# Rounding nine weight chunks by a casting DMA of GpSimd, and starting four tiles of a down projection before a wait

## The reference, cut to what matters

```python
u = rmsnorm(h, mix_norm)
(aq, ak, av, gq, gk, gv, gr, g_low, gate_a, gate_b) = split(u @ w_in)
ya = window_sink_attention(aq, ak, av, sinks)           # softmax over blocks of 64 tokens
yb = gated_linear_attention(gq, gk, gv, log_a)          # a recurrence in chunks of 64
...
h = h + 0.5 * (silu(x @ w_gate) * (x @ w_up)) @ w_down  # 1024 -> 2816 -> 1024
```

## Time and profile before

| what | value |
|---|---|
| median of 3 runs | 1890.07 us |
| the profiled execution | 1890.56 us, span 1888.4 us |
| TensorE matmul busy | 98% of the span |
| VectorE, ScalarE, GpSimd busy | 65%, 43%, 5% |
| granted TensorE clock | 0.999 of full speed |
| DMA | 110 GB/s on average |

### The profile page before, as it was taken

How to read it: one execution, slowest core, us unless ns; L and a number is a source line. 1 busy time by engine, 2 the same in 40 slices (tenths; PEclk the granted TensorE clock), 3 DMA queues, 4 the chain that set the end, 5 groups by cost and what they waited for, 6 DMA issues and landing times.

```text
span 1888.4 us, 27498 instructions
## 1 busy us (share of the span) xinstructions
PE 1858.1 (98%) x11675; PEld 1606.4 (85%) x11675; DVE 1225.5 (65%) x1498; ACT 820.8 (43%) x1154; POOL 99.5 (5%) x105
## 2 busy tenths in 40 slices
PE   8999999999999999999999999999999999999998
PEld 3788878877888888799999999888778878998998
DVE  8667743458657567587694785764554567695784
ACT  4544543336435345264452454554333354352442
POOL 0021000002000000000100100000000000110100
PEclk9999999999999999999999999999999999999999
DMA  8454423222244333222543443211122233544441
GB/s 337 154 187 157 156 80 123 89 89 68 73 123 123 98 120 95 90 74 72 139 123 107 115 121 101 90 59 46 68 83 95 90 95 95 134 112 123 116 121 66
DMA packets 66344, 208.12 MB, mean 110 GB/s; under 512 B 4512, under 2 KB 32704, under 8 KB 51376
## 3 DMA queue, kind: packets, MB, share of 16 engines
q1 hardware_dynamic: 36656, 173.55, 26.9%
q0 software_dynamic: 29568, 32.84, 8.5%
HBM read 204.27 MB, written 2.10 MB: 109 GB/s over the span
## 4 chain that ended last, share of the span: by engine, by line
PE 92%; DVE 5%; ACT 2%; issue 1%; DMA 0%; POOL 0%; DVEq 0%; ACTq 0%; POOLq 0%
PE PS L833 90%; PE PS L1000 1%; DVE W_lo L2305 1%; ACT W_hi L1675 0%; DVE N L2959 0%; ACT N L1675 0%; DVE N L2954 0%; DVE T L3037 0%; DVE N L2918 0%; DVE N L2949 0%; ACT H_hi L1675 0%; ACT X L1675 0%; DMA X<-in_xT 0%; DVE N L2333 0%; PE PS L1292 0%
## 5 line engine op out<-in xcount | busy, mean ns | idle before, releaser
L1675 ACT ACTIVATE W_hi<-W_raw 128x2048 fp32r<-128x2048 f32 (+3 forms) x158 | 289.9, 1836 | 351.4 <-PE PS L833 328.2
L833 PE MATMUL PS<-H_hi,W_hi 128*128 128x512 f32 (+2 forms) x1296 | 428.0, 345 | 5.4 <-POOL H_lo L801 2.4
L833 PE MATMUL PS<-H_lo,W_hi 128*128 128x512 f32 (+2 forms) x1296 | 425.8, 344 | 0.0
L833 PE MATMUL PS<-H_hi,W_lo 128*128 128x512 f32 (+2 forms) x1272 | 422.9, 347 | 0.0
L2305 DVE TENSOR_TENSOR W_lo<-W_raw,W_hi 128x2048 fp32r<-128x2048 f32 (+2 forms) x107 | 236.9, 2214 | 102.6 <-ACT W_hi L1675 102.4
L833 PEld LDWEIGHTS PS<-H_hi,W_hi 128*128 128x128 f32 x1296 | 236.1, 188 | 40.8 <-issue 4.4
L833 PEld LDWEIGHTS PS<-H_lo,W_hi 128*128 128x128 f32 x1296 | 235.6, 188 | 30.3 <-issue 0.7
L833 PEld LDWEIGHTS PS<-H_hi,W_lo 128*128 128x128 f32 x1272 | 232.0, 188 | 28.9 <-issue 0.7
L833 PE MATMUL PS<-G_hi,W_hi 128*128 128x264 f32 (+2 forms) x736 | 215.7, 332 | 2.1 <-DVE G_lo L3024 1.6
L833 PE MATMUL PS<-G_lo,W_hi 128*128 128x264 f32 (+2 forms) x736 | 216.2, 333 | 0.0
L833 PE MATMUL PS<-G_hi,W_lo 128*128 128x264 f32 (+2 forms) x736 | 215.6, 332 | 0.0
(11 more groups left out here) (362 smaller groups left out, 3456.7 us busy)
## 6 DMA issues: line engine op xcount, KB each, us to landing
W_raw<-in_wts SPq DMA_DIRECT2D x116, 1024.0 KB, 4.9
ring<-in_wada POOLq DMA_DIRECT2D x32, 512.0 KB, 3.9
W_raw<-in_wdown SPq DMA_DIRECT2D x12, 1024.0 KB, 5.0
W_raw<-in_wts POOLq DMA_DIRECT2D x45, 256.0 KB, 4.4
W_raw<-in_wdown SPq DMA_DIRECT2D x12, 768.0 KB, 4.4
W_raw<-in_wdown SPq DMA_DIRECT2D x12, 640.0 KB, 4.2
A_high<-in_wada SPq DMA_DIRECT2D x6, 1024.0 KB, 18.4
W_raw<-in_wdown SPq DMA_DIRECT2D x12, 384.0 KB, 4.8
```

Source lines behind the costliest of these rows:

```text
L833: return nc.tensor.matmul(*a, **kw)
L1675: return nc.scalar.activation(*a, **kw)
```

## The change

Two parts. First, chunks +5 to +13 of the second mixer get their `W_hi` from a DMA that GpSimd issues: it reads the chunk from HBM a second time and casts to float32r on its way into `W_hi`. It waits for the same use of chunk c-2 as ScalarE did. ScalarE only counts. VectorE waits for the landing of the load and of the casting DMA, then subtracts as before, at the same place of its order. Second, in the first part of each down projection the first four tiles of the second output tile of chunk q=1 are computed ahead of the wait for `hidden_lo`.

```diff
+BACK_CAST = range(5, len(BACK))
...
+        def is_cast(c):
+            return c.step == 0 and c.base - st["back"].c in BACK_CAST
+        def pool_weights(d):
+            return sem(f"pool_weights{d % 2}"), 16 * (d // 2 + 1)
+        def cast_at(c):
+            return pool_weights(fast_before("up3", 0) + c.base - st["back"].c - BACK_CAST.start)
         def summed_at(name, n):
-            done = fast_before(name, n)
-            return sem(f"first_sum{done % 2}"), 16 * (done // 2 + 1)
+            return pool_weights(fast_before(name, n) + (len(BACK_CAST) if name == "up3" else 0))
...
             pool.wait_ge(sem("mix_const_loaded"), 64)
+            for k in BACK_CAST:
+                c = At(st["back"].c + k)
+                pool.wait_ge(w_used, (c + -1).n)
+                pool.dma_start(W_hi[:, c.odd, :], wts[BACK[k][2]]).then_inc(cast_at(c)[0], 16)
             first_sums("up3")
...
                 products(1, 0, 0, size - 2)
+                ahead = size - 2 if part == 0 else 0
+                if ahead:
+                    products(1, 1, 0, ahead)
                 pe.wait_ge(sem("hidden_lo"), HIDDEN[name] + p1)
                 products(0, 0, size - 2, size)
                 products(0, 1, size - 2, size).then_inc(w_used, 1)
                 products(1, 0, size - 2, size)
-                products(1, 1, 0, size).then_inc(w_used, 1)
+                products(1, 1, ahead, size).then_inc(w_used, 1)
...
             def split(c, size, free=False):
+                if is_cast(c):
+                    act.sem_inc(w_hi, 1)
+                    return
...
             def split(c, size, narrow=None):
+                if is_cast(c):
+                    dve.wait_ge(w_loaded[c.odd], (c.half + 1) * 16)
+                    dve.wait_ge(*cast_at(c))
+                    vector.tensor_tensor(W_lo[:, c.odd, 0:size], W_raw[:, c.odd, 0:size],
+                                         W_hi[:, c.odd, 0:size].bitcast(FP32), ALU.subtract).then_inc(w_lo, 1)
+                    return
```

## The result

The changed kernel takes 1902.3 us (median of 4 runs, 1901.22 to 1903.36) against 1890.2 us of the kernel before (4 runs, 1890.05 to 1890.62): a ratio of 1.0063, with a 95% interval of 1.005 to 1.0076. The forecast was 1898.7 us with a range of 1893 to 1914. So the sign and the case were right, and the size was 3.6 us short: the time lies inside the range, but above the 1895 to 1901 us that the prediction gave to its own case. The profiled execution took 1901.22 us with a span of 1899.4, which is 11.0 us more than the span before.

What follows compares the result with a forecast made beforehand. TensorE, busy 98% of the span, was taken as the bound, so its standing still adds in full. Terms 7.7 + 0.2 + 0.7 = 8.6 us slower gave 1898.7 us against the median, range 1893 to 1914.

Steps and rivals of the forecast that it cites:

- the sign: Whole kernel: slower by more than 0.2% (3.8 us), chance 0.86.
- the case: Window attention: VectorE's wait for casts delays TensorE; landing 4.4 to 6.5 us, total 1895 to 1901 us, chance 0.6.
- Landing of the cast, 5.4 us: GpSimd's 1 MB casting DMAs: 2.4 us + 3.0 us per MB, from a line through its plain DMAs.
- the accumulating DMA: Rival for the casts: they run at its pace, 10.4 us per 1 MB, in full 1922 us; slower cast chance 0.26.
- The three window waits, 2.45 + 2.5 + 2.7 = 7.7 us: Window attention, chunks +6, +7, +8: TensorE turns probabilities later because VectorE's subtraction waits for the cast.
- ScalarE's 0.8 and the greater part of its 0.6: Chunk +8: TensorE's waits for ScalarE, PRW's later 0.8 us and LV's 0.6, disappear inside the new wait, bringing nothing.
- Chunk +5 covered, its 1.33 us wait stays: VectorE reaches this split late with its own work, hiding latencies up to 7.5 us; its subtraction still holds TensorE up.
- VectorE's waits: Second mixer: VectorE waits for a DMA before nine subtractions less one.
- Linear attention +0.2: Five chunks there: waits lie among idle times; at the tightest, +10, AM ends slightly late, costing 0.2 us.
- Part two, +0.7: Down projections: filling the G_lo wait wins 1.7 us once, waits at q=2 lose 2.4 over three networks.
- the cover that I reckoned for q=2: Down projection: splitting q=2 needs 3.3 us; its cover falls from 5.6 to 2.8 us, so TensorE stands 0.8 us.
- The sum, 8.6 us: Whole kernel slower by 7.7 us window attention, 0.2 linear attention and 0.7 down projections.

Runs made afterwards that it cites:

- the later splits: All nine casts, no tiles moved ahead, VectorE's splits of chunks +6 to +8 two steps later: 1889.29 us, ratio 0.9993 against the kernel before.
- The version with two tiles: Kernel before with two tiles moved ahead of the G_lo wait in place of four, no casts: 1888.97 us, ratio 0.9993.
- part one alone: Kernel before plus all nine casts, down projection's tiles in their old order: 1902.1 us, ratio 1.0063.
- the tiles alone: Kernel before plus the four tiles moved ahead in the down projection, no chunk cast: 1891.19 us, ratio 1.0007.
- the fewer idle products: Changed kernel plus 8, 8 and 14 unread products at TensorE's waits behind chunks +6, +7 and +8: 1900.12 us, ratio 1.005 against the kernel before.

## Why the prediction was right, and where it fell short

- **The case.** Right: latency from product to subtraction is too long for the place where VectorE waits, TensorE's turning is queued behind it, and nothing behind wins it back. Changing that order alone, by the later splits, takes away the whole loss, and casting where VectorE has slack costs nothing.
- **Landing of the cast, 5.4 us.** Measured 5.1 as the median. The line through plain DMAs of GpSimd was a good price, SyncE's 4.9 a still nearer one; that the accumulating DMA would be the measure is refuted. The Trainium skill, "DMA: Bandwidth & Descriptors", section "Anatomy of one DMA — SWDGE (gpsimd) path", gives 4.4 us as an estimate (2.0 us plus the bytes over 436 GB/s). The quickest of the 75 casts landed after 4.88 us, so the rows were the better guide.
- **The three window waits, 2.45 + 2.5 + 2.7 = 7.7 us.** Measured 1.9 + 1.9 + 2.15 = 6.0. Each was too large by some 0.6: waking 0.3 for 0.4, landing 5.1 for 5.4, and 1.3 for 1.6 from the subtraction to the turning. That ScalarE's 0.8 and the greater part of its 0.6 would vanish within the third wait without gain was right.
- **Chunk +5 covered, its 1.33 us wait stays.** Right, even with its landing of 5.9 us.
- **VectorE's waits.** It was to wait for a cast before eight of nine subtractions, and waited before six: besides +5, also +12 and +13 had landed when VectorE came to them.
- **Linear attention +0.2.** It was nothing. The casts there landed a little sooner than I had put them.
- **Part two, +0.7.** Measured +0.63, with waits of 0.64, 0.50 and 0.64 us at q=2 where I had 0.8. The version with two tiles confirms the cover that I reckoned for q=2.
- **The sum, 8.6 us.** By its own terms it came to 0.63 + 5.95 = 6.6. It failed in the sentence "whatever makes TensorE stand still is added to the time in full": added is more than that. A wait of 3.2 us was followed by 10.2 us at the lower level of the clock, which cost another 4.1 us, two thirds of what all three waits cost together. And 0.8 us came at the last store. Both terms are missing in the sum, the first also in the list of what would show me wrong. The range held the result because it reached towards a slower cast, not because of the reason that applied: that the total came out inside it is in part luck.

The slow stretches in the window attention agree in their price: 10.2 us cost 4.1; 3.4 us cost 1.4 to 1.6 (in three kernels, behind the second wait); the 6.8 us of part one alone cost 3.1. Elsewhere the price is another. In two of the twelve traces, those of the tiles alone and of the fewer idle products, the clock was low for 3.4 us from 435.4 and 435.7 us on, long before the window attention, behind a wait of 2.2 us for H_lo. The kernel before has that wait too, and full clock behind it. There the stretch cost 0.2 us. The window 435.5 to 439 us of the kernel with fewer idle products shows VectorE, the third pair of columns, busy almost throughout:

```profile
435.50:439.00 3.50, 3.50 (x11) 2.67 (x10) 3.39 (x6) 2.96 (x6) 2.29 (x2) 0.53 0.00 0
```

That TensorE does not set the pace there, and so loses little, is argued from this row and not tested.

What stays open: why the clock falls behind a wait of 1.9 us in some runs and not in others, and why an instruction packet delays some transfers and not others. In the traces of two kernels no slow stretch followed a wait that idle products filled in whole or in half, but neither bought what I expected of its time, the one for its own overshoot and a slow stretch at another wait, the other for two late casts. That the last term explains all five of its runs is only argued, since the casts of just one were read.

## What to carry to other kernels

When an operation moves from a near engine to a DMA with more latency, move its consumer too: behind whatever the bounding engine waits for on the same queue. Two steps in VectorE's order turned +12.1 us into −1.1, the latter within the noise of no change. Price a new wait of TensorE by more than its length, for its clock may be lower for a while behind it (here 4.1 us on top of 6.0), and where work is moved ahead of a wait, move only as much as fills it, because each product moved is taken from the cover of the chunk that follows.

## What I had not expected of the hardware

- TensorE's granted clock went from 2.4 to 1.2 GHz (1.00 to 0.50) behind waits as short as 1.9 us in the middle of dense work, for 3.4 to 10.2 us, in some runs and not in others. In two traces it stayed up where idle products filled at least half of the wait.
- A casting DMA is hardly dearer than a plain one: 1 MB landed in 5.1 us, SyncE's plain load of the same chunk in 4.9.
- Where a single 16 KB packet of an instruction queue fell into a cast of 1 MB and no other transfer did, 6 of 18 landed 1.1 to 2.3 us later than the usual 5.1. An 8 KB packet went with landings of a 128 KB store 0.7 to 1.0 us later than 1.95, in 6 traces of 6. Nine instructions more on GpSimd brought such a packet into the last two microseconds of the kernel, and eight did not.
